# State copies moved on SyncE's queue, from in front of the last two w_out parts to behind the last feed-forward weights

## What is computed

```python
h = rmsnorm(x);  z = h @ w_in                       # conv, dilated attention, block-sparse attention, gates
m = g0 * conv_branch + g1 * dilated_branch + g2 * moba_branch
x = x + m @ w_out
x = x + square(relu(rmsnorm(x) @ w_ff1)) @ w_ff2
```

```python
ke = concat([kbuf, dk], axis=1);  new_kbuf = ke[:, -wb:]      # likewise the values
```

## Time and profile before

| what | value |
|---|---|
| time, median of 3 runs (lowest, highest) | 539.73 us (538.67, 539.84) |
| profiled execution, from its first to its last instruction | 541.1 us |
| TensorE busy | 484.2 us, 89% of the span |
| VectorE, ScalarE, GpSimd busy | 68%, 43%, 29% |
| DMA: bytes moved, mean rate | 130.87 MB, 242 GB/s |
| mean granted TensorE clock | 0.946 of full speed |

### The profile page before, as it was taken

One profiled execution on the slowest core, in us unless ns is written; L12 is line 12 of the kernel. 1 busy time (PEld: TensorE's weight loads), 2 busy tenths in 40 slices (PEclk: granted clock), 3 DMA queues, 4 the chain that ended last, 5 costly groups with the idle time before them and its releaser, 6 DMA issues.

```text
span 541.1 us, 9293 instructions
## 1 busy us (share of the span) xinstructions
PE 484.2 (89%) x3669; PEld 443.0 (82%) x3669; DVE 367.8 (68%) x477; ACT 233.2 (43%) x428; POOL 156.5 (29%) x85
## 2 busy tenths in 40 slices
PE   3959996979859989978966998999999999999997
PEld 1848895869759769957654788899999999999997
DVE  3146999999999774799441685797777774444440
ACT  6344564225346424404175335744544443434330
POOL 4555563756547524702110506300000000000000
PEclk9969999789898969979996899999999999999999
DMA  9983775476936846716989926598898999699900
GB/s 284 381 289 117 270 275 177 180 271 230 354 111 213 260 156 222 250 74 253 342 337 351 311 89 223 161 306 303 246 354 294 282 305 282 234 254 306 294 11 20
DMA packets 86235, 130.87 MB, mean 242 GB/s; under 512 B 2806, under 2 KB 82076, under 8 KB 83620
## 3 DMA queue, kind: packets, MB, share of 16 engines
q1 hardware_dynamic: 82669, 93.99, 54.5%
q0 software_dynamic: 2992, 35.95, 17.7%
q10 hardware_dynamic: 543, 0.51, 0.3%
HBM read 128.05 MB, written 24.74 MB: 282 GB/s over the span
## 4 chain that ended last, share of the span: by engine, by line
PE 56%; DVE 21%; DMA 9%; issue 9%; ACT 3%; POOL 1%; SPq 1%; ACTq 0%; DVEq 0%
PE ps L943 34%; DVE ca L1362 6%; DVE kv L1326 5%; DMA raw<-in_w_in 5%; DMA kv<-in_cache_v,pidx 3%; PE ps L631 3%; PE ps L632 3%; PE ps L633 3%; DVE stdq L1317 3%; PE ps L760 2%; PE ps L821 2%; PE ps L852 2%; DVE sm L1330 1%; DMA raw<-in_w_out 1%; PE ps L692 1%
## 5 line engine op out<-in xcount | busy, mean ns | idle before, releaser
L575 POOL TENSOR_TENSOR rawlo<-raw,whi 128x1024 fp32r<-128x1024 f32 x53 | 131.4, 2493 | 113.5 <-ACT whi L1029 113.4
L631 PE MATMUL ps<-acts,whi 128*128 128x264 f32 x424 | 130.9, 309 | 18.3 <-POOL rawlo L575 12.6
L632 PE MATMUL ps<-acts,whi 128*128 128x264 f32 x424 | 125.7, 297 | 0.0
L633 PE MATMUL ps<-acts,rawlo 128*128 128x264 f32 x424 | 125.2, 295 | 0.0
L631 PEld LDWEIGHTS ps<-acts,whi 128*128 128x128 f32 x424 | 85.8, 202 | 26.1 <-POOL rawlo L575 14.7
L1622 DVE TENSOR_TENSOR ws<-fraw,ws 128x1024 fp32r<-128x1024 f32 x64 | 78.1, 1221 | 40.2 <-ACT ws L1224 40.1
L943 PE MATMUL ps<-as,ws 128*128 128x264 f32 x768 | 94.7, 284 | 0.0
L943 PEld LDWEIGHTS ps<-as,ws 128*128 128x128 f32 x768 | 93.3, 188 | 0.2
L943 PE MATMUL ps<-hs,ws 128*128 128x264 f32 x768 | 93.2, 284 | 0.0
L943 PEld LDWEIGHTS ps<-hs,ws 128*128 128x128 f32 x768 | 92.9, 188 | 0.1
L632 PEld LDWEIGHTS ps<-acts,whi 128*128 128x128 f32 x424 | 85.8, 202 | 0.1
(11 more groups left out here) (226 smaller groups left out, 523.2 us busy)
## 6 DMA issues: line engine op xcount, KB each, us to landing
fraw<-in_w_ff SPq DMA_DIRECT2D x32, 1024.0 KB, 8.1
raw<-in_w_in SPq DMA_DIRECT2D x14, 1536.0 KB, 8.2
out_dk_s<-in_state_dil_k SPq DMA_DIRECT2D x8, 1023.5 KB
out_dv_s<-in_state_dil_v SPq DMA_DIRECT2D x8, 1023.5 KB
raw<-in_w_out SPq DMA_DIRECT2D x2, 1536.0 KB, 8.8
ebias<-bias_rows SPq DMA_DIRECT2D x4, 512.0 KB, 7.6
out_dk_s<-in_state_dil_k SPq DMA_DIRECT2D x8, 255.5 KB
out_dv_s<-in_state_dil_v SPq DMA_DIRECT2D x8, 255.5 KB
```

The costliest lines, as they stand in the source:

```text
L575: pool.tensor_tensor(raw_unit(u, rawlo), raw_unit(u), whi[u % WR][:, :, :].bitcast(F32), ALU.subtract).then_inc(wlo_ready, 1)
L631: pe.matmul(out, hi, acts[0][:, k], start=k == 0, stop=False)
L632: pe.matmul(out, hi, acts[1][:, k], start=False, stop=False)
L633: return pe.matmul(out, lo, acts[0][:, k], start=False, stop=k == KD - 1)
```

## The change

Ten transfers, `copy_state(0)`, `copy_state(1)` and the two of 508 KB, are taken from between `load(17)` and `load(18)` and put behind `load_and_store(3, False)`, ahead of the stores of columns 6 and 7. They stay on SyncE's queue, with the same sources, targets and semaphore. Nothing else differs.

```diff
-            copy_state(0)
-            copy_state(1)
-            for src, dst in ((state[0][0], state[0][2]), (state[0][1], state[0][3])):
-                a = src.rearrange("l n w h e -> (l n) (w h e)")[:, P:P * P]
-                b = dst.rearrange("l n w h e -> (l n) (w h e)")[:, 0:(P - 1) * P]
-                sp.dma_start(b, a).then_inc(copied, 16)
             load(NCH - 2)
             load(NCH - 1)
...
             load_and_store(3, False)
+            copy_state(0)
+            copy_state(1)
+            for src, dst in ((state[0][0], state[0][2]), (state[0][1], state[0][3])):
+                a = src.rearrange("l n w h e -> (l n) (w h e)")[:, P:P * P]
+                b = dst.rearrange("l n w h e -> (l n) (w h e)")[:, 0:(P - 1) * P]
+                sp.dma_start(b, a).then_inc(copied, 16)
             for m in (6, 7):
                 store_y(m)
```

## The result

| what | before | after |
|---|---|---|
| median of the comparison (lowest, highest; 4 runs each) | 539.2 us (536.37, 539.84) | 547.41 us (544.52, 554.15) |
| ratio, 95% interval | | 1.0138 (1.0084 to 1.0193) |
| span of the profiled run | 541.1 us | 552.3 us |
| forecast | | 543.2 us (540.9 to 544.5) |

The kernel became slower, as forecast, by about 7 us where 3.5 had been forecast; the time lies outside the range.

A forecast was written before the change was run, and what follows sets the result against it. TensorE, busy 89% of the span, was taken as the bound. Nothing gained at w_out and copies outlasting the last outputs add 3.5 us to the 539.73 us median: 543.2 us, range 540.9 to 544.5.

The forecast's parts named there:

- Removed at w_out: worth nothing.: Before the last w_out parts: SyncE and DMA queues idle, so taking the copies away gains 0, at most 1.0 us.
- Added at the end.: Behind the sixth output column: the copies outlast the last outputs and lengthen the span by 3.5 us (1.2 to 4.6).
- issue to the first copy packet: After the sixth output column: 1.0 us from the copies' issue at 521.42 to their first packet at 522.4.
- the ten copies: At the end: 6.28 MB move for 20.4 us (19.0 to 21.5), ending at 542.8.
- outputs behind them: Last two outputs wait on eight engines for the 508 KB copies, then take 0.9 us (0 if they slip in between).
- to the end of the span: From the last output's last packet to the span's end: 0.85 us.
- tail longer by: Stretch from issue of the last output column to the span's end; forecast as span +3.5 us (+1.2 to +4.6).
- because the sequence, the sizes and the empty queues are the same at 522: Reason for giving the copies at the end the 20.4 us they took in front in the kernel before.
- Hidden: Rival: copies hide behind the last two output columns if through within about 17.3 us; 539.7 us, chance 0.10.
- Held at issue: Rival: the copies' issues stall, so SyncE reaches the last two outputs only at 542.8; 545.3 us, chance 0.05.
- The copies did hold the w_out parts: Rival: copies slowed the w_out parts through memory; 1.0 us back there, same cost at the end, 542.2 us, chance 0.05.

The follow-up runs named there:

- no_copies: The kernel before with the ten copies left out altogether: 539.42 us against 540.34 for the kernel before (ratio 0.9983).
- act_out: The changed kernel with the last two output columns stored from ScalarE's queue, not SyncE's: 549.83 us against 540.17 for the kernel before (1.0129).
- half_end: The kernel before with only `copy_state(0)` (2.62 MB) moved to the end: 538.77 us against 540.09 for the kernel before (1.0012).
- two_end: The kernel before with both copy groups (5.24 MB) moved to the end, the 508 KB pair left in front: 541.25 us against 540.17 (1.0023).
- front_more: The kernel before with a third group, `copy_state(5)`, moved from the feed-forward to the front: 546.75 us against 540.17 (1.012).
- big_first: The changed kernel with the first group's 1023.5 KB copies issued ahead of its 255.5 KB ones: 547.33 us against 540.09 for the kernel before (1.0169).

## Why the prediction was right in sign and wrong in size

**"Removed at w_out: worth nothing."** Right in mechanism. SyncE's time and the queue were idle there (the queue for 1.8 to 5 us), and the chain still stands 6.7 to 6.9 us on the same transfer; no_copies shows that even leaving the copies out wins hardly anything. The gain is 0.5 us, inside the bound of 1.0, where 0 was taken. Its cause was not isolated: in most runs without copies in front the part lands in 6.7 to 6.9 us, yet in 7.2 in act_out, and in half_end and two_end, which leave some of the copies in front, in 6.8 and 6.7.

**"Added at the end."** Right in mechanism, step by step: issue right behind the sixth column, ten issues in 7.3 us (7.6 forecast), no hold of the last outputs, packets past the last output's issue, and SyncE's waits for `copied` and the last output as the last ones. Of the pair of 508 KB never more than eight packets are under way at once. The sizes:

| term | forecast | after |
|---|---|---|
| issue to the first copy packet | 1.0 | 1.35 |
| the ten copies | 20.4 (19.0 to 21.5) | 22.0 (four profiles 21.2 to 22.0) |
| outputs behind them | 0.9 | 0.83 |
| to the end of the span | 0.85 | 0.9 |
| tail longer by | 3.5 (1.2 to 4.6) | 5.4 (four profiles 4.6 to 5.4) |

The mis-sized term is the copies' length, above the upper bound of 21.5 in this profile and at it in the others (21.2 to 21.6); with the later first packet it makes up the 1.9 us that are missing in this profile (1.6 + 0.35). One small slip is in the last term: 539.7 + 0.45 is 540.15 and not 540.25, though the trace of before does have its last packet end at 540.25. The step that failed is the sentence "because the sequence, the sizes and the empty queues are the same at 522": the same sequence ran at 349 GB/s in front and 332 at the end, and its packets took longer there. The Trainium skill's page "DMA: Bandwidth & Descriptors", which the forecast weighed as a rival, would have these bytes through in 16.4 us by its fit, an estimate, in time to hide; the runs show 21.2 to 22.0, so here the trace was nearer, and still too low.

**The rivals.** *Hidden* decides at 17.3 us by the forecast, 16.6 by the terms measured; half_end (9.4 us of copies) and two_end (17.7) show both sides of it. *Held at issue* did not happen. *The copies did hold the w_out parts* is false for this queue, though the 0.5 us are its sign; front_more shows the point from which it becomes true.

**What took the time out of the range.** With the terms as measured, -0.5 and +5.0, the same sum gives 539.73 + 4.5 = 544.2 us, still inside the range. The measured 547.4 is 3 us above that. The forecast had no term for the runs' own scatter: it took the three runs of before, 1.2 us from end to end, as the precision of a run, and 0.2% as what can be told from no change. The 87 runs of before lie within 19.5 us, and in the profiles two waits of GpSimd alone move the first half by 14; the medians of after were above before's by 8.2, 6.4, 6.6 and 4.3. A range that allowed for it would have had to reach several microseconds further, on both sides.

## What to carry to other kernels

A transfer that nothing reads is free only while it ends before the last output: put it right behind the last loads and ahead of waits for results, and compare its length with the time that is left before the last output. Before moving it away from a load, look whether its packets were through when that load was issued; if they were, there is nothing to win there. And take the length of a transfer from the stretch in which it will run, or widen the range by what the nearest rows differ.

## What the runs showed of the hardware

- The same stretch of some hundred products took 13.0 us at full granted clock in one execution and 21.0 us at a mean of 0.84 in another execution of the same kernel, with a stand of TensorE of 6.0 us before the clock was at 0.50. Two waits of GpSimd for VectorE, 1.9 or 9.35 us and 5.4 to 5.8 or 9.3 us, sort the first halves from 278 to 292 us into three groups. One profile is one draw.
- The same ten copies from DRAM to DRAM took 20.4 to 20.7 us in six profiles where they ran in front or behind weight loads, and 21.2 to 23.0 in seven at the end; not for the order of their sizes (big_first).
- Stores of outputs on another engine's queue did not get past copies in flight: their last packets started as the copies ended, after 546.4.
- Rows of 65 KB on half the engines or pieces of 4 KB on all of them made 0.6 to 1.4 us of difference for 1.04 MB.
